# An encoder trunk on one core: weight casts of the branch merge on ScalarE, and 24 branch tiles written out

## The reference

```python
branches = jnp.stack([out_a, out_b, out_c], axis=2)
proj = jnp.einsum('btiw,iwd->btid', branches, w_branch)
gates = jax.nn.sigmoid(gate_in.reshape(b, t, N_BRANCH, D_MODEL))
y = jnp.sum(gates * proj, axis=2) @ w_out
```

## Time and profile before

| | |
|---|---|
| median of three runs | 3328.78 us (3324.94 to 3329.90) |
| the profiled execution | 3329.66 us, its span 3328.1 us |
| TensorE busy | 2959.1 us, 89% of the span |
| VectorE busy | 1594.1 us, 48% |
| ScalarE busy | 720.1 us, 22% |
| chain that ended last | PE 75%, DVE 10%, issue 4%, DVEq 4%, ACT 3% |
| mean granted clock of TensorE | 0.948 |
| branch matmuls of the merge, layer 0 | 933 to 1032 us |
| branch matmuls of the merge, layer 1 | 2567 to 2666 us |

### The profile page before, as it was taken

The page is one execution under the profiler, slowest core; times in us unless marked ns, Lnnn a source line. Parts: engine busy times, 40 slices in busy tenths (PEclk is TensorE's granted clock), DMA queues, the critical chain, the costliest instruction groups (busy, mean ns, idle before and its releaser), DMA issues.

```text
span 3328.1 us, 69908 instructions
## 1 busy us (share of the span) xinstructions
PE 2959.1 (89%) x26572; PEld 2724.6 (82%) x26572; DVE 1594.1 (48%) x2968; ACT 720.1 (22%) x1777; POOL 248.5 (7%) x430
## 2 busy tenths in 40 slices
PE   4989998898979989999969899988897898899997
PEld 3967776888879869999968777778897897799997
DVE  3434553466664236554253344525666742455533
ACT  1023332222221230000011333322222122200001
POOL 1112111100000010000001111110000000000000
PEclk8989998999989999999988998989999999999999
DMA  3433334422143312332224333352221521233221
GB/s 107 128 100 111 90 100 85 130 63 65 51 125 112 89 41 83 88 88 76 81 63 130 93 92 102 94 133 84 66 65 52 159 83 51 64 89 88 85 77 56
DMA packets 420780, 294.59 MB, mean 89 GB/s; under 512 B 38560, under 2 KB 386240, under 8 KB 419968
## 3 DMA queue, kind: packets, MB, share of 16 engines
q1 hardware_dynamic: 397056, 225.19, 24.4%
q0 software_dynamic: 23424, 65.36, 5.9%
HBM read 234.28 MB, written 56.23 MB: 87 GB/s over the span
## 4 chain that ended last, share of the span: by engine, by line
PE 75%; DVE 10%; issue 4%; DVEq 4%; ACT 3%; DMA 2%; ACTq 1%; POOLq 1%; POOL 0%; SPq 0%
PE PS L690 30%; PE PS L754 9%; PE PS L1055 6%; PE PS L996 6%; PE PS L668 4%; PE PS L644 2%; ACT U L1311 2%; PE PS L1200 2%; DVE WLO L1796 2%; PE PS L921 2%; PE PS L838 1%; PE PS L803 1%; PE PS L1034 1%; ACT U L1314 1%; DMA U<-in_rwkv_g_dram 1%
## 5 line engine op out<-in xcount | busy, mean ns | idle before, releaser
L690 PE MATMUL PS<-U_r,WHI 128*128 128x272 f32 x2656 | 487.2, 295 | 66.9 <-DVEq L1797 31.7
L1786 DVE CAST WHI<-ring 128x1024 fp32r<-128x1024 f32 (+2 forms) x292 | 189.4, 649 | 655.1 <-PE PS L690 488.0
L690 PEld LDWEIGHTS PS<-U_r,WHI 128*128 128x128 f32 x2656 | 395.9, 192 | 76.4 <-issue 47.2
L1314 ACT COPY U<-PS 128x272 f32<-128x272 f32 (+9 forms) x774 | 269.3, 371 | 870.3 <-PE PS L1055 143.5
L690 PE MATMUL PS<-brT_r,WHI 128*128 128x272 f32 x1728 | 360.0, 290 | 1.9 <-ACTq L1695 1.9
L690 PE MATMUL PS<-U_r,WLO 128*128 128x272 f32 x1696 | 355.8, 292 | 0.0
L690 PE MATMUL PS<-hT_r,WHI 128*128 128x272 f32 x1696 | 350.2, 288 | 0.0
L1796 DVE TENSOR_TENSOR WLO<-ring,WHI 128x1024 fp32r<-128x1024 f32 (+2 forms) x292 | 332.2, 1138 | 22.8 <-issue 0.9
L754 PE MATMUL PS<-U_r,WHI 128*128 128x272 f32 x832 | 272.5, 327 | 34.3 <-ACT U L1314 34.3
L996 PE MATMUL PS<-U_r,WHI 128*128 128x272 f32 x768 | 238.4, 310 | 50.3 <-POOLq L403 27.4
L690 PE MATMUL PS<-brT_r,WLO 128*128 128x272 f32 x1344 | 278.2, 288 | 0.0
(11 more groups left out here) (320 smaller groups left out, 4453.9 us busy)
## 6 DMA issues: line engine op xcount, KB each, us to landing
ring<-in_w_in_dram SPq DMA_DIRECT2D x126, 512.0 KB, 4.1
ring<-in_w_ffn_in_dram SPq DMA_DIRECT2D x88, 512.0 KB, 3.8
ring<-in_w_ffn_out_dram SPq DMA_DIRECT2D x32, 448.0 KB, 3.3
proj_scratch<-U POOLq DMA_DIRECT2D x104, 136.0 KB, 2.0
U<-proj_scratch SPq DMA_DIRECT2D x48, 272.0 KB, 4.1
gate_scratch<-U POOLq DMA_DIRECT2D x96, 136.0 KB, 2.5
U<-gate_scratch SPq DMA_DIRECT2D x48, 272.0 KB, 2.8
ring<-in_w_branch_dram SPq DMA_DIRECT2D x48, 256.0 KB, 3.0
```

The lines of the kernel that those rows point to most:

```text
L690: ins = mm(PS[:, 2 * q + h, 0:HT], w, half(x, h), start=(first and k == 0 and n == 0), stop=(last and k == kn - 1 and n == len(terms) - 1))
L1314: return act.copy(out, in_)
L1786: copy(hi, src)
```

## The change

ScalarE takes over the 24 casts of weight units in the merge: after each tile n it casts unit n+2 from the ring into WHI, and counts it on `gt_cast`, now 17 + 24 in a layer. The sigmoid of tile n+1 stands ahead of that cast in its queue. VectorE waits for `gt_cast` in place of the tile and the ring slot, and only subtracts. The 24 tiles are written out on TensorE, ScalarE and VectorE in place of a loop of two trips, so that every unit is cast and subtracted at its own depth (4 for branch units, 8 for units of the output projection).

```diff
@@ TensorE
-                with pe.Fori(0, 2) as it:
-                    for n in range(12):
-                        dense_split(l, G_BR + n, n % 4, V_BR + n, of_branch(n % 3), it=it, per=12,
-                                    need=4 + 2 * n if n < 3 else None)
+                for n in range(N_BR):
+                    dense_split(l, G_BR + n, n % 4, V_BR + n, of_branch(n % 3), need=4 + 2 * n if n < 3 else None)
@@ ScalarE
-                with act.Fori(0, 2) as it:
-                    for n in range(12):
-                        act.wait_ge(gs_loaded[n % 4], 16 * (l * 6 + n // 4 + 1 + it * 3))
-                        f(GS[:, n % 4, :], GS[:, n % 4, :], ACT.Sigmoid).then_inc(gs_ready, 1)
+                def sigmoid(n):
+                    act.wait_ge(gs_loaded[n % 4], 16 * (l * 6 + n // 4 + 1))
+                    f(GS[:, n % 4, :], GS[:, n % 4, :], ACT.Sigmoid).then_inc(gs_ready, 1)
+
+                sigmoid(0)
+                for n in range(N_BR):
+                    if n + 1 < N_BR:
+                        sigmoid(n + 1)
+                    v = V_BR + n + 2
+                    c = unit_of(v)
+                    tile(l, G_BR + n)
+                    act.wait_ge(slot_loaded[c % RING], 16 * (l * USES[c % RING] + c // RING + 1))
+                    copy(WHI[:, v % 2, 0:depth_of(v), :].rearrange("p k n -> p (k n)"),
+                         ring[:, c % RING, 0:depth_of(v), :].rearrange("p k n -> p (k n)")).then_inc(gt_cast, 1)
@@ VectorE, gate_rest
-                    dve.wait_ge(gt_cast, l * 17 + q - 8 + it * 8)
+                    dve.wait_ge(gt_cast, l * (17 + N_BR) + q - 8 + it * 8)
@@ VectorE, merge
-                with dve.Fori(0, 2) as it:
-                    for n in range(12):
-                        i, to = n % 3, YT[:, ds(it * 4 + n // 3, 1), :]
-                        tile(l, G_BR + n, it, 12)
-                        split_unit(l, V_BR + n + 2, it, 12, depth=8 if n >= 10 else None)
-
-                        dve.wait_ge(gs_ready, l * 24 + n + 1 + it * 12)
+                for n in range(N_BR):
+                    i, to = n % 3, YT[:, n // 3:n // 3 + 1, :]
+                    v = V_BR + n + 2
+                    c = unit_of(v)
+                    hi, lo, w = (x.rearrange("p k n -> p (k n)") for x in (
+                        WHI[:, v % 2, 0:depth_of(v), :], WLO[:, v % 2, 0:depth_of(v), :], ring[:, c % RING, 0:depth_of(v), :]))
+                    dve.wait_ge(gt_cast, l * (17 + N_BR) + 17 + n + 1)
+                    tt(lo, w, hi.bitcast(F32), ALU.subtract)
+                    dve.drain().then_inc(split_done, 1)
+
+                    dve.wait_ge(gs_ready, l * 24 + n + 1)
```

More of the change, by code:

```diff
@@ new lines, in _ @@
+                for n in range(N_BR):
[8 more added lines that the diff above has]
+                    dve.wait_ge(gs_ready, l * 24 + n + 1)
+                    for h in range(2):
+                        dst = to[:, :, h * HT:(h + 1) * HT] if i == 0 else mid(half(TM[:, n % 2, :], h), HT)
+                        tt(dst, mid(PS[:, 2 * (n % 4) + h, 0:HT], HT), mid(half(GS[:, n % 4, :], h), HT), ALU.mult)
+                    dve.drain().then_inc(tile_freed_dve, 1)
+                    dve.sem_inc(gs_free, 1)
+                    if i > 0:
+                        tt(to, to, mid(TM[:, n % 2, :], T), ALU.add)
+                        dve.drain()
+                    if i == 2:
+                        y_hi = YH[:, n // 3:n // 3 + 1, :]
+                        take_high(y_hi, to)
+                        dve.drain()
+                        tt(YL[:, n // 3:n // 3 + 1, :], to, y_hi.bitcast(F32), ALU.subtract).then_inc(y_ready, 1)
```

## The result

The changed kernel takes 3286.62 us (median of four runs, 3279.22 to 3294.64) against 3328.20 before: ratio 0.9877, 95% interval 0.9852 to 0.9902. The direction was right; the size and the range were wrong.

A forecast was written before the change was run, and what follows sets the result against it. TensorE bounds the whole span, VectorE the merges; relieving VectorE wins 14.0 us in layer 0 and 14.6 in layer 1, with clock and stalls at zero 28.5 us, giving 3300.5 us, range 3294 to 3312.

The forecast's parts named there:

- The clock behind the merge: TensorE after layer 0's merge: a shorter wait may give up to 1.8 us; set to zero against one or two stalls.
- the low clock at the start of layer 0's merge: TensorE from tile 2 in layer 0: the low clock was charged at 13 x 0.24 = 3.1 us.
- The range: Whole kernel: 3294 to 3312 us, from bounds of 26 to 31 us won, clock included, and most of rival A.
- What bounds the merge, and the casts as its price: Merge: VectorE full at 10.7 to 10.8 us a group, TensorE needs 9.0; moving casts saves VectorE 13.1 us a layer.
- The hand-over: TensorE to ScalarE to VectorE to TensorE: VectorE starts about 0.95 us after a tile; split ready at 5.85 of 6.0 us.
- the straight line: ScalarE's 128x512 cast, estimated at 0.63 us by a line through two measured operations, 1.052 and 0.658 us.
- Rival A: Merge: the hand-over between engines becomes the bound, 9.9 us a group, 6.8 us a layer won, 3315 us; chance 0.11.
- Rivals B and C: Merge: B, ring transfers bind, 3317 us, chance 0.03; C, ScalarE reloads tables, 3343 us, 0.04 with anything else slower.
- The gaps: VectorE in the merge: one wait for two and constant addresses save 0 to 0.5 us a group, 4 us a layer.
- TensorE's floor in layer 0: Merge of layer 0: TensorE's tiles and closing chain end at 1019.1 us, so at most 15.0 us can be won.
- the middle: Merge savings midway between bounds: 14.0 us in layer 0, 14.6 in layer 1, together 28.6 us.
- a shorter wait for the last y: End of layer 0's merge: TensorE waiting less for the last y may give back up to 1.8 us of clock.

The follow-up runs named there:

- experiment 3: Against the kernel before: only the loops written out, at true depth, casts still on VectorE; 3313.44 us, ratio 0.9963.
- experiment 8: Against the changed kernel: three more casts of y on VectorE before the last y subtraction; 3291.31 us, 0.9911 of the kernel before.
- experiment 9: Against the changed kernel: five ScalarE casts for one at every third tile, plus three more y casts at the end; 3318.49 us, 0.9962 of before.
- experiment 4: Against the kernel before: only the casts moved to ScalarE, the loops of two trips kept; 3288.11 us, ratio 0.989.

## Why the prediction was right, and where it was wrong

In the merge the mechanism was right; the sum failed mainly on two of its terms. The clock behind the merge stood at zero and gave 6.0 us, and the low clock at the start of layer 0's merge stood at 3.1 us and cost 1.6. The range, built from the merge and 1.8 us of clock, left too little room for the first.

**What bounds the merge, and the casts as its price: right.** VectorE was full, its group fell from 10.81 us to 9.04 (forecast 9.0 to 9.3), and TensorE took over as the bound. The casts alone gave 38 us.

**The hand-over: right, a little cautious.** ScalarE's small cast took 0.62 us against the 0.63 of the straight line. The chain has 0.11 us from the end of tile 22 to ScalarE's cast and 0.02 from its end to VectorE (1008.26, 1008.37 + 1.06, 1009.45), so 0.75 in place of 0.95 for a small cast. Rival A did not come, but only 0.29 us were left. Rivals B and C did not come either: TensorE never waited on a split for want of data, and between 928.72 and 1012.45 us ScalarE loads no table.

**The gaps: the upper end.** I allowed 0 to 0.5 us a group, with 0.3 of it for one wait in place of two; experiment 3, which keeps both waits, shows 0.5 by the written-out loop alone. Its own forecast had 0.1 to 0.3, against the prediction's own bound.

**TensorE's floor in layer 0: mis-sized by 1.5 us.** I charged tiles 2 to 23 with 13 x 0.24 = 3.1 us of low clock, the whole deficit of the stretch 944 to 957. That stretch describes the old execution, where the clock was low for 5.6 us from 944.52 on, after 3.67 us of idle time. Now TensorE idled 2.94 us and was at full clock again some 3 us after 943.30: 1.6 us lost (the 21 tiles took 64.96 us, at 3.01 each they would need 63.3). The step took a property of one execution as one of the work. Its ceiling was 15.0 us; 16.1 were won. It isn't fixed in the changed kernel either: in layer 1 of its third profile the clock was low for 6.2 us there (mean 0.50 in 2555 to 2561), and that merge took 90.92 us where the other five took 89.5 to 89.7. For layer 1 the middle was 14.6, and 14.9 were won in the first profile.

**The clock behind the merge: set to zero, and it was 6 us.** I saw the 0.89 after the merge, priced it at up to 1.8 us in one layer, and set it to zero against "one or two small stalls". There were no stalls, and it was 3.0 us a layer by the means, on the first output tile and at an idle time that I hadn't looked at. Why the change brings it is not known: the reason I gave, a shorter wait for the last y, is what experiment 8 speaks against, and experiment 9 bears out on one first output tile of two. So this is 6 of the 13 us missed, and the 1.8 us that I had priced were less than a third of it; the merges, with 31.5 in place of 28.6 by the means, are 3.

**The range: too narrow by its construction.** It added up the bounds of the merge, and 1.8 us for the clock. But stages of unchanged code moved by up to 3.2 us between executions, the runs of the changed kernel spread by 15 us (3279.2 to 3294.6), and three runs of before within 5 us had hidden that: later ones on one chip spread from 3314.9 to 3343.4. Of the remaining 4 us of the median no cause was found; the means of the last projection and attention of layer 1 and of its low-rank stage are 3 us lower each in the changed kernel, on scatter of the same size.

## What to carry to other kernels

An engine that is full in one stage, while another idles beside it, is worth relieving even at a price: the cast costs 0.62 us on ScalarE in place of 0.42 on VectorE, and the merge is 15% shorter. Work out the new bound in full before summing the savings, since the second half of a change may then buy little (13 us alone, 2 by the medians on top of the other). Bound a clock deficit by what the changed schedule does, not by what the old one did, and take the range's width from repeated profiles of the untouched stages.

## What the runs showed of the hardware

An idle time of TensorE of the same length, between the same instructions, is followed by the low clock in one kernel and not in another (1.9 us: 6 of 6 layers against 0 of 6), and one of 2.3 us passed without a fall in both layers of the kernel with the longer wait alone. The length of the idle time alone does not tell.

On VectorE a loop whose addresses and wait values hang on its register costs idle time between the instructions of work. Ahead of the multiplication it was 0.37 to 0.38 us at i = 0 and 0.24 at i = 1 with the loop (before, experiment 4), and 0.19 to 0.20 with it written out (experiment 3, the changed kernel); a group of three tiles became 0.5 us shorter with no instruction of work removed. Addresses and wait values were not tried one by one.
